# mLSTM stage of a hybrid block: projection two steps behind the scores, second half in two pieces

## The reference, cut to what matters

```python
y_sb = _head_rmsnorm(_merge_heads(y_sb), sb_norm_w[i], SB_HEADS) * jax.nn.silu(sb_z)
...
num = jnp.einsum('bhcls,bhcsv->bhclv', scores, v) + carry_scale[..., None] * jnp.einsum('bhcld,bhcvd->bhclv', q, c_prev)
h = num / jnp.maximum(jnp.abs(den), jnp.exp(-m_t))[..., None]
...
y_ml = jax.nn.sigmoid(ml_o) * _merge_heads(y_ml)
y_ml = _head_rmsnorm(y_ml, ml_norm_w[i], ML_HEADS) * jax.nn.silu(ml_z)
y = jnp.concatenate([y_sb, y_ml], axis=-1) @ w_out[i]
h = h + _rmsnorm(y, post_norm_w[i])
```

## Time and profile before

| | us |
|---|---|
| median of 3 runs (1868.65 to 1871.02) | 1869.4 |
| the profiled execution | 1869.05 |
| its span | 1867.2 |
| last matmul of stage c ends (from the span's start) | 1601.59 |
| first matmul of stage c | 1302.58 |
| idle of TensorE between stages c and d | 11.09 |
| TensorE busy, whole span | 1778.0 (95%) |
| VectorE / ScalarE / GpSimd busy | 1128.3 / 998.2 / 694.5 |

### The profile page before, as it was taken

The page is one execution under the profiler, slowest core; times in us unless marked ns, Lnnn a source line. Parts: engine busy times, 40 slices in busy tenths (PEclk is TensorE's granted clock), DMA queues, the critical chain, the costliest instruction groups (busy, mean ns, idle before and its releaser), DMA issues. The chain is left out here.

```text
span 1867.2 us, 28230 instructions
## 1 busy us (share of the span) xinstructions
PE 1778.0 (95%) x8972; PEld 1448.1 (78%) x8972; DVE 1128.3 (60%) x1768; ACT 998.2 (53%) x2045; POOL 694.5 (37%) x956
## 2 busy tenths in 40 slices
PE   5999999999789999999999999997799999699998
PEld 4888888878468888888888888885688888588887
DVE  4531213554469888878897888786565665333333
ACT  4421212322257787877777878775777775311111
POOL 2100000000136777777777777776234444100000
PEclk9999999999999999999999999997799999899999
DMA  4657787121294647364846476532445453422221
GB/s 163 167 168 202 227 204 195 50 90 45 96 282 136 201 129 243 109 196 128 231 139 175 153 210 195 155 118 83 154 159 183 155 167 121 156 77 77 76 76 45
DMA packets 193386, 277.13 MB, mean 148 GB/s; under 512 B 66716, under 2 KB 128412, under 8 KB 184184
## 3 DMA queue, kind: packets, MB, share of 16 engines
q1 hardware_dynamic: 189592, 259.95, 45.9%
q0 software_dynamic: 3248, 12.62, 1.9%
q10 hardware_dynamic: 432, 3.15, 0.5%
HBM read 187.41 MB, written 88.26 MB: 148 GB/s over the span
## 5 line engine op out<-in xcount | busy, mean ns | idle before, releaser
L966 PE MATMUL b_late<-w_split,spare 128*128 128x512 f32 x1536 | 436.8, 412 | 1.0 <-ACT b_p_out L1048 0.6
L748 POOL TENSOR_TENSOR b_a_lo<-b_aT,b_a_hi 128x512 fp32r<-128x512 f32 (+1 forms) x320 | 367.0, 1147 | 25.6
L1120 DVE TENSOR_TENSOR_SCAN b_buf<-b_y,b_buf 128x511 f32<-128x511 f32 (+2 forms) x320 | 357.9, 1118 | 9.2
L966 PEld LDWEIGHTS b_late<-w_split,spare 128*128 128x128 f32 x1536 | 265.6, 190 | 43.4 <-issue 1.9
L1130 DVE SCALAR_TENSOR_TENSOR b_buf<-b_buf,b_y 128x512 f32<-128x512 f32 (+2 forms) x320 | 189.2, 591 | 113.7 <-PE b_y L928 111.5
L746 POOL CAST b_a_hi<-b_aT 128x512 fp32r<-128x512 f32 (+1 forms) x320 | 181.8, 568 | 202.7 <-PE b_o L942 156.0
L522 PE MATMUL a_po<-uT_hi,w_split 128*128 128x512 f32 x768 | 241.0, 395 | 2.1 <-DVE w_split L395 2.1
L1034 ACT ACTIVATE b_buf<-b_y 128x512 f32<-128x512 f32 (+2 forms) x320 | 171.3, 535 | 84.9 <-PE b_y L922 83.4
L1025 ACT ACTIVATE b_aT<-b_turned 128x512 f32<-128x512 f32 (+1 forms) x320 | 170.4, 533 | 74.7 <-POOL b_a_lo L748 71.4
L1036 ACT ACTIVATE b_buf<-b_buf 128x512 f32<-128x512 f32 (+2 forms) x320 | 181.9, 568 | 10.2
L904 PE MATMUL b_turned<-b_ident,b_buf 128*128 128x128 f32 x1088 | 172.3, 274 | 1.3 <-ACT b_aT L1025 1.3
(11 more groups left out here) (227 smaller groups left out, 3417.3 us busy)
## 6 DMA issues: line engine op xcount, KB each, us to landing
spare<-u_pair SPq DMA_DIRECT2D x61, 1024.0 KB, 5.4
proj_n<-b_p_out SPq DMA_DIRECT2D x64, 256.0 KB, 5.7
c_gates<-proj_n SPq DMA_DIRECT2D x16, 768.0 KB, 4.5
w_raw<-in_w_in POOLq DMA_DIRECT2D x5, 2048.0 KB, 10.2
x_in<-in_x SPq DMA_DIRECT2D x16, 512.0 KB, 4.2
qk_hi<-stage_hi SPq DMA_DIRECT2D x32, 256.0 KB, 2.6
qk_lo<-stage_lo SPq DMA_DIRECT2D x32, 256.0 KB, 3.2
u_pair<-uT_hi SPq DMA_DIRECT2D x16, 512.0 KB, 4.1
```

What stands on the lines that cost most here:

```text
L748: nc.gpsimd.tensor_tensor(lo[:, cols], raw, hi[:, cols].bitcast(F32), ALU.subtract).then_inc(lo_done, 1)
L966: mm = pe.matmul(late[:], u_in[f % US][:, u_part, k, :], w[:, k, :], start=(i == 0), stop=(i == PASSES - 1))
L1120: nc.vector.tensor_tensor_scan(down, y[u % YS][:, 1:keys][:, ::-1], down, b[:, keys - 1:keys], ALU.add, ALU.subtract).then_inc(log_done, 1)
```

## The change

Five things change together.

1. LAG goes from 3 to 2 and TURN_LAG from 2 to 1: tile c-1 is turned and tile c-2 projected in step c. The post norm and the residual stay three steps behind, under a new constant POST_LAG.
2. On TensorE the second projected half is done in two pieces of 12 matmuls; the first turning stands between them, the second behind them. Each turning waits only for its own half of y.
3. VectorE's `norm_heads` is split: the attention half stays where it was, the mLSTM half (with `ml_gated`) moves behind `numerator(c, 0)`. Both `low` follow directly behind it; `post` moves to the front of the step.
4. ScalarE does both `high` one behind the other after `carry(c, 0)`. GpSimd does the post norm's root first.
5. `c_num` gets two buffers.

```diff
-        num = sb("c_num", [P, H, DV + 3])
+        num = [sb(f"c_num{s}", [P, H, DV + 3]) for s in range(2)]
...
-        NORM_LAG, TURN_LAG, LAG = 1, 2, 3
-        FIRST = 2 * LAG
+        NORM_LAG, TURN_LAG, LAG, POST_LAG = 1, 1, 2, 3
+        FIRST = 4
...
-            for c in range(TOK, TOK + LAG):
+            for c in range(TOK, TOK + POST_LAG):
...
-                    if has(c, LAG + 1):
-                        store(d - 1, 1 - sd)
+                if has(c, POST_LAG + 1):
+                    store(c - POST_LAG - 1, s)
...
             def turn(t, s, half):
-                until(pe, sb_y_done, t + 1)
-                until(pe, ml_gated, t + 1)
+                until(pe, (sb_y_done, ml_gated)[half], t + 1)
                 until(pe, yT_lo_done, 2 * t + half)
...
-            def project(d, s, n):
+            def project(d, s, n, ks=range(KT)):
...
-                for k in range(KT):
+                for k in ks:
...
-                mm.then_inc(out_done, 1)
+                if KT - 1 in ks:
+                    mm.then_inc(out_done, 1)
...
                     score(c, s, 0)
-                if has(c, TURN_LAG):
-                    turn(c - TURN_LAG, st, 0)
                 if has(c, LAG):
                     project(c - LAG, sd, 0)
                 if has(c, 0):
                     score(c, s, 1)
                     combine(c, s, 0)
+                if has(c, LAG):
+                    project(c - LAG, sd, 1, range(KT // 2))
+                if has(c, TURN_LAG):
+                    turn(c - TURN_LAG, st, 0)
+                if has(c, LAG):
+                    project(c - LAG, sd, 1, range(KT // 2, KT))
                 if has(c, TURN_LAG):
                     turn(c - TURN_LAG, st, 1)
-                if has(c, LAG):
-                    project(c - LAG, sd, 1)
                 if has(c, 0):
                     combine(c, s, 1)
...
-                if has(c, TURN_LAG):
-                    high(c - TURN_LAG, st, 0)
                 if has(c, NORM_LAG):
                     square(c - NORM_LAG, (s - NORM_LAG) % 2)
...
                     carry(c, 0)
+                if has(c, TURN_LAG):
+                    high(c - TURN_LAG, st, 0)
...
+                if has(c, POST_LAG):
+                    post_norm(c - POST_LAG)
                 if has(c, NORM_LAG):
                     head_norms(c - NORM_LAG, (s - NORM_LAG) % 2)
-                if has(c, LAG):
-                    post_norm(c - LAG)
-                    add_residual(c - LAG, (s - LAG) % 2)
+                if has(c, POST_LAG):
+                    add_residual(c - POST_LAG, (s - POST_LAG) % 2)
...
-                until(dve, ml_gated, c)
+                until(dve, ml_gated, c - 1)
...
-                if has(c, TURN_LAG):
-                    low(c - TURN_LAG, st, 0)
+                if has(c, POST_LAG):
+                    post(c - POST_LAG, (s - POST_LAG) % 2)
                 if has(c, NORM_LAG):
                     mean_squares(c - NORM_LAG)
                 if has(c, 0):
                     weights_times_scores(c, 1)
                 if has(c, NORM_LAG):
-                    norm_heads(c - NORM_LAG, (s - NORM_LAG) % 2)
+                    norm_attention(c - NORM_LAG, (s - NORM_LAG) % 2)
                 if has(c, 0):
-                    numerator(c, 0)
+                    numerator(c, s, 0)
+                if has(c, NORM_LAG):
+                    norm_mlstm(c - NORM_LAG, (s - NORM_LAG) % 2)
+                if has(c, TURN_LAG):
+                    low(c - TURN_LAG, st, 0)
                 if has(c, TURN_LAG):
                     low(c - TURN_LAG, st, 1)
                 if has(c, 0):
-                    numerator(c, 1)
+                    numerator(c, s, 1)
                     divide(c, s)
-                if has(c, LAG):
-                    post(c - LAG, (s - LAG) % 2)
```

More of the change, by code:

```diff
@@ L1652, in square @@
                 until(act, ml_y_done, b + 1)
-                nc.scalar.activation(squares[:, SB_WIDTH:], num[:, :, 0:ML_DIM], ACT.Square, scale=ML_DIM ** -0.5)\
+                nc.scalar.activation(squares[:, SB_WIDTH:], num[s][:, :, 0:ML_DIM], ACT.Square, scale=ML_DIM ** -0.5)\
                     .then_inc(squares_done, 1)
@@ L1749, in mean_squares, with norm_attention @@
                         .then_inc(ss_done, 1)
-            def norm_heads(b, s):
+            def norm_attention(b, s):
                 until(dve, rstd_done, b + 1)
@@ L1757, in norm_heads, with norm_mlstm @@
                                         ALU.mult).then_inc(scaled_done, 1)
+            def norm_mlstm(b, s):
                 until(dve, silu_done, b + 1)
@@ L1760, in norm_heads @@
                     i = nc.vector.scalar_tensor_tensor(
-                        out=y[s][:, SB_WIDTH + h * ML_DIM:SB_WIDTH + (h + 1) * ML_DIM], in0=num[:, h, 0:ML_DIM],
+                        out=y[s][:, SB_WIDTH + h * ML_DIM:SB_WIDTH + (h + 1) * ML_DIM], in0=num[s][:, h, 0:ML_DIM],
                         scalar=rstd[:, SB_HEADS + h:SB_HEADS + h + 1],
@@ L1765, in norm_heads, with numerator @@
                 i.then_inc(ml_gated, 1)
-            def numerator(c, p):
+            def numerator(c, s, p):
                 u = 2 * c + p
@@ L1770, in numerator @@
                 until(dve, intra_done, u + 1)
-                until(dve, ml_gated, c)
-                nc.vector.tensor_tensor(num[:, 2 * p:2 * p + 2, 0:DV], carried[p][:, :, 0:DV], intra[:, :, 0:DV],
+                until(dve, ml_gated, c - 1)
+                nc.vector.tensor_tensor(num[s][:, 2 * p:2 * p + 2, 0:DV], carried[p][:, :, 0:DV], intra[:, :, 0:DV],
                                         ALU.add).then_inc(num_done, 1)
@@ L1784, in divide @@
                 until(dve, num_done, 2 * c + 2)
-                dens = num[:, :, ML_DIM]
+                dens = num[s][:, :, ML_DIM]
                 nc.vector.scalar_tensor_tensor(out=den[:, 0, :], in0=dens, scalar=-1.0, in1=dens,
@@ L1797, in divide @@
                     i = nc.vector.scalar_tensor_tensor(
-                        out=num[:, h, 0:ML_DIM], in0=num[:, h, 0:ML_DIM], scalar=den[:, 2, h:h + 1],
+                        out=num[s][:, h, 0:ML_DIM], in0=num[s][:, h, 0:ML_DIM], scalar=den[:, 2, h:h + 1],
                         in1=gates[s][:, 2 * GROUP + h * ML_DIM:2 * GROUP + (h + 1) * ML_DIM],
```

## The result

| | before | after |
|---|---|---|
| median, us (4 runs each) | 1869.03 | 1890.47 |
| ratio | | 1.0113 (1.0101 to 1.0125) |
| profiled span | 1867.2 | 1887.7 |

The change costs 21.4 us.

A forecast was written before the change was run, and what follows sets the result against it. TensorE was taken to bound the steady mLSTM steps, busy 17.00 of 17.00 us. Added waits and stage ends of 34.8 plus clock falls of 17.8 made 52.6 on 1869.05: 1922 us, range 1902 to 1938.

The forecast's parts named there:

- (g): TensorE's clock: falls to the slow level at every other wait, 6.5 x 2.74 = 17.8 us.
- (a): Second turning on TensorE: waits 2.56 us each full step for the moved gating and `low` 0; step 19.54 against 17.00.
- (e): Start of the stage: turnings now precede combine 1; combine 1 of step 2 at 1352.6, of step 15 at 1606.6.
- (f): End of the stage: 29.8 us from combine 1 of step 15 to the last matmul, near 1636.4; +34.8 us overall.
- (b): First turning on TensorE: waits 0 to about 0.5 us for the attention half, inside a longer wait; cost 0.
- (c): Next projection: needs high and low of the tile just turned, some 1.6 us, covered by 2.47 of matmuls; cost 0.
- (d): Post, residual addition, x loads, stores: engines have 6 us and more idle per step; cost 0, perhaps a few us once.
- rival 1: TensorE's clock holds through the waits: 1904 us; chance 0.22.
- Rival 3: Faster: no wait at the second turning, period 17.0, about 1864.4 us if step 1 isn't held up either; chance 0.02.

The follow-up runs named there:

- gating first: The changed kernel with the mLSTM half gated in front of numerator 0 again: 1874.88 us, ratio 1.0036 against the kernel before.

## Why the prediction was right in direction and wrong in size

The forecast was 31.5 us too high. (g) is 17.8 of it and the waits and the two ends of the stage are 15.7; 2 us went the other way (the idle around the stage, and the median against the profiled execution).

- **(a) right in mechanism, wrong in size; this is the step that failed.** Period forecast 19.54, measured 18.54. The whole difference is the gating, priced at 2.18 us from the earlier trace rows and measured at 1.14. The row's four instructions had stood beside GpSimd's gate; the change moves them away from it, and I carried the price along. Over thirteen steps this is 13.0 us, with 2.3 more in the start (e) and 0.4 in the end (f). The runs with GpSimd's work moved on and off the gating show it from both sides.
- **(g) failed too, at least in part through (a).** No fall of the clock in the 14 waits of 1.3 us: 17.8 us too many. The forecast wait would read 2.40 in the profile (2.56 less 0.16). At the nearest that was run, 2.04 to 2.13 us, the clock fell after ten of fourteen waits; at 3.2 us, with three of thirteen. So some falls are likely at 2.40, but how many is not shown. The price per fall was too high (2.74 against 1.6).
- **(b) right.** The attention half is ready at 1473.71 + 1.31 = 1475.02, the first turning starts at 1475.58 in its turn. No wait in the full steps.
- **(c), (d) right.** No wait for `c_yT_lo` before the projection in full steps, none for a load in the stage. But (d) saw only that GpSimd's addition has room; it did not ask what it would run beside. As it fell, it was done before the gating began.
- **(e) nearly.** Combine 1 of step 2 was forecast at 1352.6 and starts at 1351.02, on a stage that begins 0.71 later (1303.29 against 1302.58): 2.3 early. Step 2's gating is 1.0 of it. A clock that rose sooner, in the scores at 1333.79, is another 1.15: combine and scores took 1334.85 - 1331.28 = 3.57 us instead of 4.72. Step 1's gating was short too (1.13), but `c_carried` ended at 1327.63 instead of 1326.08, which took most of that back.
- **(f) right.** From combine 1 of step 15 (1592.00) to the last matmul's end (1633.33 - 11.92 = 1621.41) are 29.4 us against 29.8. The idle before the next stage is 11.92 instead of 11.09.
- Sum: last matmul 34.8 forecast, 1621.41 - 0.71 - 1601.59 = 19.1 measured; with 0.8 more of idle behind the stage and 0.7 ahead of it this is 20.6, within 0.1 us of the 20.5 between the spans.
- **The rivals.** The case that came was rival 1, clock held, with a smaller (a). Its 1904 was 14 us off, nearly all of it by the gating's price in (a). Rival 3 did not come, but its point of decision, `c_carried` soon enough, is what the later runs built on.

## What to carry to other kernels

When an instruction is moved, price it in its new place: look at its shortest, median and longest duration, not only the mean, and ask who worked beside it, and who will. A dependent step that ran in another engine's shadow is cheap only while it stays there; moved behind the wait that made the shadow, it goes on the path in full. When a pipeline is shortened, the links that come late in the step (here the scaled carry behind the gates' activations) must come sooner, or the lag saved comes back as a wait in every step, as it did here.

## What the runs showed of the hardware

- A VectorE instruction with two SBUF operands stands still while a GpSimd operation on SBUF operands runs: 0.34 us became 1.40 beside a 1.34 us one (kernel before) and 2.49 beside a 2.46 us one (gating first); four of them took 4.33 us beside both. Instructions with one operand in PSUM were not stretched (two states 0.60 with the addition beside them and without). The GpSimd operation was hardly longer (1.34 against 1.29 us). The Trainium skill, page "SBUF — State Buffer", section "Who interferes with whom", says that a VectorE instruction with two SBUF inputs contends with a GpSimd instruction that reads SBUF; the traces agree.
- TensorE's clock fell to 1.2 GHz (granted clock 0.50) after ten of fourteen idle stretches of 2.04 to 2.13 us, after none of fourteen of 1.3 us, and with three of thirteen of 3.2 us. The idle stretch of 2.2 us ahead of the last tile's first turning came with a fall in two of six kernels. Why the longer idle fell less often is not shown.
